# One fused decoder block on one core: the order of a values' product and a block of probability transposes on TensorE

## What is computed

```python
def block(args):
    q_i, i = args
    s = jnp.einsum('bhqd,bhkd->bhqk', q_i, kh).astype(jnp.float32)
    qpos = i * Q_BLOCK + jnp.arange(Q_BLOCK)
    s = jnp.where(kpos[None, :] <= qpos[:, None], s, NEG_INF)
    prob = jax.nn.softmax(s, axis=-1).astype(vh.dtype)
    return jnp.einsum('bhqk,bhkd->bhqd', prob, vh)
o = lax.map(block, (q_blocks, jnp.arange(n_blk)))
```

## Time and profile before

| what | value |
| --- | --- |
| median of 3 runs | 1112.12 us (1110.82 to 1112.43) |
| time of the profiled execution | 1112.55 us |
| span of its instructions | 1110.8 us |
| TensorE matmul busy | 1093.1 us (98% of the span) |
| VectorE, ScalarE, GpSimd busy | 77%, 71%, 38% |
| chain that ended last | PE 92%, DVE 3%, ACT 2% |
| attention blocks | about 290 to 354 us of the span |

### The profile page before, as it was taken

How to read it: one execution, slowest core, us unless ns; L and a number is a source line. 1 busy time by engine, 2 the same in 40 slices (tenths; PEclk the granted TensorE clock), 3 DMA queues, 4 the chain that set the end, 5 groups by cost and what they waited for, 6 DMA issues and landing times.

```text
span 1110.8 us, 17828 instructions
## 1 busy us (share of the span) xinstructions
PE 1093.1 (98%) x5488; PEld 915.5 (82%) x5488; DVE 859.6 (77%) x1231; ACT 786.9 (71%) x1270; POOL 421.4 (38%) x477
## 2 busy tenths in 40 slices
PE   7999999999999999999999999999999999999998
PEld 7988888878778888888888888888888888888787
DVE  3535532278765468999999999999999999999865
ACT  6644433357654343888889898889888988888772
POOL 1120000015276003355555555555555555554400
PEclk9999999999999999999999999999999999999999
DMA  7422422012401259999999999999999999999642
GB/s 250 153 76 76 139 87 76 27 59 72 157 1 69 103 217 375 358 377 378 389 394 388 395 392 389 390 390 395 394 395 396 397 393 395 390 391 357 192 152 76
DMA packets 72130, 291.60 MB, mean 263 GB/s; under 512 B 15187, under 2 KB 20598, under 8 KB 47126
## 3 DMA queue, kind: packets, MB, share of 16 engines
q1 hardware_dynamic: 52672, 254.13, 57.0%
q0 software_dynamic: 18768, 34.79, 12.4%
q10 hardware_dynamic: 646, 2.12, 0.5%
HBM read 284.61 MB, written 42.07 MB: 294 GB/s over the span
## 4 chain that ended last, share of the span: by engine, by line
PE 92%; DVE 3%; ACT 2%; POOL 1%; issue 1%; DMA 0%; ACTq 0%; POOLq 0%; DVEq 0%
PE bank L2060 11%; PE bank L2062 11%; PE bank L2061 10%; PE bank L1750 7%; PE bank L1787 6%; PE bank L1788 6%; PE bank L1791 6%; PE bank L2088 5%; PE bank L2087 5%; PE bank L2086 5%; PE bank L2025 5%; PE bank L1741 2%; PE bank L1942 1%; PE bank L2158 1%; PE bank L2160 1%; PE bank L2159 1%
## 5 line engine op out<-in xcount | busy, mean ns | idle before, releaser
L1622 DVE TENSOR_TENSOR arena_r<-arena,win_r 128x1024 fp32r<-128x1024 f32 x252 | 292.0, 1221 | 21.8 <-ACT win_r L1082 19.9
L1082 ACT ACTIVATE win_r<-arena 128x1024 fp32r<-128x1024 f32 x252 | 246.5, 1068 | 0.5 <-DMA resid<-in_w_exp_up 0.5
L2060 PE MATMUL bank<-win_r,work_r 128*128 128x512 f32 x512 | 206.5, 403 | 0.6 <-issue 0.6
L2061 PE MATMUL bank<-win_r,x_low_r 128*128 128x512 f32 x512 | 199.5, 390 | 0.0
L2062 PE MATMUL bank<-arena_r,work_r 128*128 128x512 f32 x504 | 197.4, 392 | 0.0
L1602 DVE TENSOR_TENSOR arena_r<-arena,hT_r 128x1024 fp32r<-128x1024 f32 x128 | 150.5, 1218 | 0.5 <-ACT hT_r L1090 0.5
L733 POOL DMA_INDIRECT moe_sum<-ya,sidx x64 | 110.0, 1719 | 103.7 <-ACT ya L1118 88.8
L1787 PE MATMUL bank<-arena_r,hT_r 128*128 128x512 f32 (+2 forms) x320 | 121.8, 381 | 2.3 <-DVE win_r L1222 2.1
L1791 PE MATMUL bank<-win_r,hT_r 128*128 128x512 f32 (+2 forms) x320 | 121.2, 379 | 0.0
L1788 PE MATMUL bank<-arena_r 128*128 128x512 f32 (+2 forms) x320 | 121.2, 379 | 0.0
L2062 PEld LDWEIGHTS bank<-arena_r,work_r 128*128 128x128 f32 x504 | 94.6, 188 | 21.7
(11 more groups left out here) (321 smaller groups left out, 2211.2 us busy)
## 6 DMA issues: line engine op xcount, KB each, us to landing
arena<-in_w_exp_down SPq DMA_DIRECT2D x64, 1024.0 KB, 12.8
arena<-in_w_exp_gate SPq DMA_DIRECT2D x63, 1024.0 KB, 8.6
arena<-in_w_exp_up SPq DMA_DIRECT2D x63, 1024.0 KB, 13.1
win<-in_w_in SPq DMA_DIRECT2D x8, 2048.0 KB, 7.7
win<-in_w_o SPq DMA_DIRECT2D x2, 2048.0 KB, 7.7
arena<-in_w_ple_gate SPq DMA_DIRECT2D x2, 2048.0 KB, 15.2
arena<-moe_sum SPq DMA_DIRECT2D x7, 512.0 KB, 7.0
win<-in_mla_w_qb SPq DMA_DIRECT2D x4, 576.0 KB, 4.0
```

What stands on the lines that cost most here:

```text
L1082: act.activation(gu_hi[n % 2][:, :, cols], raw[:, :, cols], ACT.Copy).then_inc(gu_hi_r, 1)
L1622: dve.tensor_tensor(low_[:, :, cols], raw[:, :, cols], gu_hi[n % 2][:, :, cols].bitcast(F32), ALU.subtract).then_inc(gu_lo_r, 1)
L2060: pe.matmul(b_, x_hi[:, k, :], w_hi, start=(k == 0), stop=False)
L2061: pe.matmul(b_, x_lo[:, k, :], w_hi, start=False, stop=False)
```

## The change

In a step whose transposes belong to a 512 wide block, the values' product (of the block before it) is issued ahead of the transposes; in all other steps the order stays. Nothing is added or removed, and the other engines' programs are the same.

```diff
-                if 1 <= s <= NA:
+                def probs_T():
                     n = s - 1
...
                     last.then_inc(pt_done, 1)
-                if s >= 2:
+
+                def probs_V():
                     n = s - 2
...
                     last.then_inc(pv_done, 1)
+
+                wide = 1 <= s <= NA and head_block(s - 1)[1] == NT - 1
+                if s >= 2 and wide:
+                    probs_V()
+                if 1 <= s <= NA:
+                    probs_T()
+                if s >= 2 and not wide:
+                    probs_V()
```

## The result

The changed kernel took 1113.37 us (median of 22 runs, 1112.44 to 1114.36), the kernel before 1111.55 us in 22 runs beside it (1110.63 to 1112.88): a ratio of 1.0015, 95% interval 1.0008 to 1.0021, which is +1.7 us (0.9 to 2.3; the two medians are 1.82 apart). The forecast was +1.73 on a median of 1112.12 us.

The account below looks back on a forecast made before the run. TensorE was taken to bound attention and experts, so only when it leaves the attention counts. Terms 0.22 - 0.22 + 1.10 + 0.63 = 1.73 us on the 1112.12 us median gave 1113.8 us, range 1111.8 to 1115.4.

Parts of the forecast that it names:

- (a): Heads 2 to 6, one wide block each: the moved product waits for ScalarE's copy; next scores 0.22 us later, 1.10 in all.
- The restart: Extra time of a product starting after a wait, at eight places: 0.11 us each, bounds nothing to two 0.19 weight loads.
- (b): Head 0's wide block: the same delay as in heads 2 to 6, 0.22 us.
- (c): Head 1: the earlier product lets VectorE's chain, and TensorE's transposes behind it, move forward; -0.22 us in place of +0.22.
- (d): Last block: the 384 wide product moved ahead delays the transposes, ScalarE's last copy and the last product; +0.63 us.
- dearer: Rival, chance 0.25: one or both weight loads of 0.19 us exposed at eight moved products; sum 2.4 to 3.9 us.
- hidden restart: Rival, chance 0.10: TensorE pulls weight loads ahead at the moved products, no extra start time; sum 0.85 us, 1113.0 us.
- The filled gap: Rival, chance 0.05: the product finds its copy ready, up to 0.22 us fits each of seven gaps; -1.5 us, 1110.6.
- The return by VectorE in every head: Rival, chance 0.05: VectorE gives time back in every head, not only head 1; -0.9 us, 1111.2 us, faster.

Follow-up runs that it names:

- the run with the early copy: Against the kernel before: ScalarE copies the 128 wide block ahead of the wide block's exponentials, and TensorE's product precedes the transposes, both in heads 0 to 6; 1110.08 us, 0.9986.

## Why the prediction was right

(a) Heads 2 to 6, 0.22 each: measured 0.21, 0.22, 0.23, 0.21, 0.21. The product started 0.05 after the copy's end. The restart, the term with the widest bounds, was 0.11 in the sum: in head 2 the product takes 309.09 - 308.77 = 0.32 in place of 0.22, so 0.10. It is the same at all eight moved products: the second instruction starts 0.21 after the first, and 0.11 after it where nothing waited. So the restart is neither hidden nor a whole load of 0.19. The Trainium skill (TensorE: Matmul & The Clock Gate, "Engine queue depths") says that TensorE's queue can pull weight loads ahead of matmuls in flight. Taken alone that would give no restart; the trace shows 0.10, with the first load starting only at 308.76, 0.04 after the end of the copy that it reads.

The prediction reads the gap before the wide transposes in head 2, 0.23, and counts it seven times. In the kernel before it is in fact 0.11 in head 0, 0.24 and 0.23 in heads 1 and 2, and 0.37 to 0.48 in heads 3 to 6. That did no harm, since the cost does not depend on the width of the gap: ScalarE's copy follows the exponentials in every head, and the product starts behind it.

(b) Head 0, 0.22: the next scores are 0.21 later, but 0.07 of it is gone one step on. I had not seen that the wide block's product of head 0 itself had waited in the kernel before: its copy ended at 295.66, and its first weight load started only at 295.71, where in other heads it starts 0.11 ahead of the product's first instruction. The copy and the product (all engines, before):

```profile
295.07 0.59 ACT L957 ACTIVATE x_low<-bank 128x512 f32<-128x512 f32 x1
...
295.74 1.13 PE L1899 MATMUL bank<-hT,x_low 128*128 128x128 f32 x8
```

Its eight instructions took from 295.74 to 296.71, 0.97, and after the change, where TensorE comes later, from 294.78 to 295.67, an undisturbed 0.89. So 0.14.

(c) Head 1, -0.22: measured -0.22 (0.14 to -0.08), and -0.22 in the run with that head alone.

(d) The last block, 0.63: measured 0.60. The last copy took 0.60, not 0.62.

The sum was 1.73, the trace gives 1.60, the times 1.7 (0.9 to 2.3). Of the 0.13 that the sum is too high, 0.08 lies in head 0, the rest in the last block and in roundings of heads 2 to 6. That the times come closer to the sum than the trace does is chance, given their interval. The time itself, 1113.8 against 1113.37, is off mainly because the kernel before has a median of 1111.55 over 22 runs and not 1112.12 as over the first three. The chance of 0.70 was on a difference within 0.2%; with 0.15% it came so, but the interval goes up to 0.21%.

Of the rivals, the dearer and the hidden restart fall with the measured 0.10. The filled gap fails for the reason given, and the run with the early copy, which supplies the condition that it lacked, gains 1.70. The return by VectorE in every head did not come in this change; where the products of all steps were moved it came in heads 3 to 6 by another piece of VectorE's work, which I had not looked for.

## What to carry to other kernels

Before work is moved into a gap on one engine, look where the thing it waits for stands in the queue of the engine that makes it: here both waits were on ScalarE, and the later one was put in front of the earlier. In heads 0 to 6, moving the producer as well turned a loss of 0.10% into a gain of 0.14%. Where the effect is of that size, read it from the length of the stage, since the profiled executions differed by up to 2.9 us before the stage began.

## What the runs showed that I had not expected

A product directly behind the mask product costs 0.05 more than one behind transposes even when its copy is done: in the run with every product ahead eight instructions took 0.95 (311.56 to 312.51), against 0.89. All of it lies between the first and the second instruction, which start 0.16 to 0.17 apart and elsewhere 0.11; the same holds for the moved products in the run of the early copy with the product ahead. A product's weight load takes 0.19, and the mask product ahead of it is followed after 0.07. That the load is not covered there is my reading, and no run tested it apart.
